# Two transitions between blocks: squares and weight-row products by halves, and both norms of the first from x and x times its row

## What is computed

```python
def rmsnorm(x, g):                      # rms_norm of the second part is the same
    y = xf * lax.rsqrt(jnp.mean(xf * xf, axis=-1, keepdims=True) + RMS_EPS)
    return (y * g.astype(jnp.float32)).astype(x.dtype)

# end of the first block: three gated branches, then
        x = x + jnp.einsum('bsd,de->bse', merged, w_out[l])
    return rmsnorm(x, final_g)

# second block, two layers
    for i in range(DEPTH_2):
        u = rms_norm(x, norm_pre[i])
        ...                             # layer 0: S5 and convolution, layer 1: gated linear attention
        x = x + rms_norm(y, norm_post[i])
    return x
```

## Time and profile before

| | |
|---|---|
| median of 3 runs | 1795.4 us |
| profiled execution | 1794.97 us, of it 1793.2 us span from the first to the last instruction |
| TensorE busy | 1667.4 us (93%) |
| VectorE busy | 928.9 us (52%) |
| ScalarE busy | 666.2 us (37%) |
| GpSimd busy | 203.4 us (11%) |
| mean granted TensorE clock | 0.972 of full speed |
| chain that ended last | PE 89%, DVE 4%, ACT 3% of the span |

### The profile page before, as it was taken

One profiled execution on the slowest core, in us unless ns is written; L12 is line 12 of the kernel. 1 busy time (PEld: TensorE's weight loads), 2 busy tenths in 40 slices (PEclk: granted clock), 3 DMA queues, 4 the chain that ended last, 5 costly groups with the idle time before them and its releaser, 6 DMA issues.

```text
span 1793.2 us, 20084 instructions
## 1 busy us (share of the span) xinstructions
PE 1667.4 (93%) x7876; PEld 1359.2 (76%) x7876; DVE 928.9 (52%) x1293; ACT 666.2 (37%) x920; POOL 203.4 (11%) x234
## 2 busy tenths in 40 slices
PE   6999989999999999989999989475989999999997
PEld 5887878878888888879988777354877778687775
DVE  4265264552246234558889937912464344453446
ACT  5333332223212223354544465216344334342442
POOL 4980000000000000031222202101000000000000
PEclk9999999999999999999999989797999999999999
DMA  8455433333333332257789838217422223132211
GB/s 245 127 155 152 131 94 94 94 117 106 99 101 94 94 98 102 95 211 161 145 216 195 162 132 187 48 62 184 131 60 64 78 71 105 48 104 60 82 48 59
DMA packets 151227, 206.75 MB, mean 115 GB/s; under 512 B 51963, under 2 KB 74987, under 8 KB 150123
## 3 DMA queue, kind: packets, MB, share of 16 engines
q1 hardware_dynamic: 131915, 173.62, 31.4%
q0 software_dynamic: 17568, 29.89, 10.2%
q10 hardware_dynamic: 1664, 2.13, 0.4%
HBM read 190.94 MB, written 14.68 MB: 115 GB/s over the span
## 4 chain that ended last, share of the span: by engine, by line
PE 89%; DVE 4%; ACT 3%; issue 2%; DMA 1%; SPq 0%; ACTq 0%; DVEq 0%
PE PS L2010 76%; PE PS L1988 2%; PE PS L2225 1%; PE PS L2277 1%; PE PS L2295 1%; PE PS L2164 1%; PE PS L2286 1%; PE PS L2131 1%; ACT XN L900 1%; DVE V L1391 1%; DMA WR<-in_conv_w_pw_dram 1%; PE PS L2194 1%; PE PS L2305 0%; DVE WL L1309 0%; PE PS L2179 0%
## 5 line engine op out<-in xcount | busy, mean ns | idle before, releaser
L2010 PE MATMUL PS<-HH,WH 128*128 128x512 f32 x1216 | 478.4, 393 | 10.5 <-issue 5.4
L2010 PE MATMUL PS<-HL,WH 128*128 128x512 f32 x1216 | 475.3, 391 | 0.0
L2010 PE MATMUL PS<-HH,WL 128*128 128x512 f32 x1216 | 475.2, 391 | 0.0
L893 ACT ACTIVATE WH<-WR 128x1024 fp32r<-128x1024 f32 x200 | 211.6, 1060 | 688.6 <-PE PS L2010 641.4
L1309 DVE TENSOR_TENSOR WL<-WR,WH 128x1024 fp32r<-128x1024 f32 x144 | 185.4, 1294 | 420.5 <-ACT WH L893 420.4
L2010 PEld LDWEIGHTS PS<-HH,WH 128*128 128x128 f32 x1216 | 229.7, 189 | 60.5 <-issue 10.8
L2010 PEld LDWEIGHTS PS<-HL,WH 128*128 128x128 f32 x1216 | 229.8, 189 | 48.2 <-issue 1.0
L2010 PEld LDWEIGHTS PS<-HH,WL 128*128 128x128 f32 x1216 | 229.4, 189 | 47.8
L2010 PE MATMUL PS<-WH,HH 128*128 128x512 f32 x384 | 153.2, 399 | 9.1 <-DVE WL L1309 4.2
L2010 PE MATMUL PS<-YH,WH 128*128 128x512 f32 x320 | 126.7, 396 | 36.0 <-DVE YL L1346 31.3
L1685 DVE SCALAR_TENSOR_TENSOR TMP<-CP,PRM,TMP 128x512 f32<-128x512 f32 x232 | 154.9, 740 | 0.0
(11 more groups left out here) (328 smaller groups left out, 1965.0 us busy)
## 6 DMA issues: line engine op xcount, KB each, us to landing
WR<-in_w_in_dram SPq DMA_DIRECT2D x96, 512.0 KB, 3.7
WR<-in_od_w_in_dram SPq DMA_DIRECT2D x32, 512.0 KB, 3.9
WR<-in_ev_w_in_dram SPq DMA_DIRECT2D x24, 512.0 KB, 3.9
WL<-in_ev_w_in_dram POOLq DMA_DIRECT2D x24, 512.0 KB, 7.5
WR<-in_ev_w_in_dram SPq DMA_DIRECT2D x32, 256.0 KB, 3.2
WR<-in_ev_w_out_dram SPq DMA_DIRECT2D x16, 512.0 KB, 4.2
WR<-in_od_w_in_dram SPq DMA_DIRECT2D x32, 256.0 KB, 3.4
WR<-in_od_w_out_dram SPq DMA_DIRECT2D x16, 512.0 KB, 3.8
```

Of the source, the lines that this page charges most:

```text
L893: act.activation(WH[:, n % RING, :, :], WR[:, n % RING, :, :], ACT.Copy).then_inc(w_hi, 1)
L2010: mm = pe.matmul(out_banks[m], st, mv, start=(kt == 0 and i == 0), stop=(kt == 2 * per - 1 and i == 2))
```

## The change

The first transition gets a second array `XG`, x times `FROW`. It is made by halves of 512 columns on VectorE (`weigh_x`), the first half of all four tiles right behind the four sums of the first half, ahead of the `split` of the unit's last chunk. ScalarE squares both X and `XG` by halves of 512, so that it has the sums of squares of x and of x times its row; both norms follow from them: X becomes XG over the root of mean(X^2) + eps, and XN1 is XG over the root of mean(XG^2) + eps * (mean(X^2) + eps). Sums of the first halves are turned into the biases of the later roots (rows 2, 3, 9 of the small array `XST`). `x1_norm` now makes both XN1 and X from `XG`, each with a reciprocal and one 128x1024 product. ScalarE's `split` (the `WH` of the next unit's chunk 0), which stood between the two norms of tile 3, now stands behind both.

The second transition squares YO by halves and makes YO times `PROW0` by halves (`weigh_y`), again with the four first halves ahead of the `split` of the last chunk; the product with rstd and the sum with X1 are one instruction. The norm of X1 is as before.

```diff
@@ -315,6 +315,10 @@
         AZ = put("AZ", "R4", [KT, SEQ])
         BZ = put("BZ", "R5", [KT, SEQ])
         XN2 = put("XN2", "R5", [TT, D])
+        XG = put("XG", "R2", [TT, D])
+        XST = put("XST", "SMALL", [10, TT])
+        JUNK1 = put("JUNK1", "YH", [TT, D])
+        JUNKG = put("JUNKG", "R5", [TT, D])
         MU = put("MU", "R6", [SEQ])
         RS = put("RS", "R6", [SEQ])
         ONES = put("ONES", "R6", [P], skip=2048)
@@ -421,6 +425,9 @@
             "o_sq", "o_std", "o_f", "o_hi", "o_lo", "rr_in", "st_done"))
         y2_zero = sem("y2_zero")
         sq5, std5, fin, fin_out, prow1_in = sem("sq5"), sem("std5"), sem("fin"), sem("fin_out"), sem("prow1_in")
+        xg_half, x_sums, x_base, x_left, x_sum = (sem(n) for n in (
+            "xg_half", "x_sums", "x_base", "x_left", "x_sum"))
+        yo_sums, yo_base = sem("yo_sums"), sem("yo_base")
         halves_done, y2_half, yg_done = sem("halves_done"), sem("y2_half"), sem("yg_done")
 
         def col(name, kt, n=1):
@@ -1083,13 +1090,34 @@
 
             load_sqrt()
             act.wait_ge(h_lo, 16)
+            def square(x, junk, row, t, sums):
+                act.activation(junk, x, ACT.Square, accum_out=XST[:, row, t:t + 1]).then_inc(sums, 1)
+
+            act.wait_ge(m_acc, 16)
+            for t in range(TT):
+                act.wait_ge(banks_dve, dve_after("w_out.0", t + 1))
+                square(X[:, t, 0:NC], XN1[:, t, 0:NC], 0, t, x_sums)
+                act.wait_ge(xg_half, t + 1)
+                square(XG[:, t, 0:NC], JUNKG[:, t, 0:NC], 1, t, x_sums)
+            act.wait_ge(x_sums, 2 * TT)
+            act.activation(XST[:, 2, :], XST[:, 0, :], ACT.Copy, scale=1.0 / D, bias=RMS_EPS).then_inc(x_base, 1)
             for t in range(TT):
                 act.wait_ge(banks_dve, dve_after("w_out.1", t + 1))
-                rms_tile(X[:, t, :], t, XN1[:, t, :], sq1, std1)
+                square(X[:, t, NC:D], XN1[:, t, NC:D], 4, t, x_sum)
+                act.wait_ge(x_sum, 2 * t + 1)
+                act.wait_ge(x_base, 2)
+                act.activation(XST[:, 6, t:t + 1], XST[:, 4, t:t + 1], ACT.Identity, scale=RMS_EPS / D,
+                               bias=XST[:, 3, t:t + 1]).then_inc(x_left, 1)
+                act.wait_ge(xg_half, TT + t + 1)
+                square(XG[:, t, NC:D], JUNKG[:, t, NC:D], 5, t, x_sum)
+                act.wait_ge(x_left, t + 1)
+                act.wait_ge(x_sum, 2 * t + 2)
+                act.activation(XST[:, 7, t:t + 1], XST[:, 5, t:t + 1], ACT.Sqrt, scale=1.0 / D,
+                               bias=XST[:, 6, t:t + 1]).then_inc(std2, 1)
+                act.activation(XST[:, 8, t:t + 1], XST[:, 4, t:t + 1], ACT.Sqrt, scale=1.0 / D,
+                               bias=XST[:, 2, t:t + 1]).then_inc(std1, 1)
                 if t == TT - 1:
                     split(1)
-                act.wait_ge(x1_done, t + 1)
-                rms_tile(X[:, t, :], t, XN1[:, t, :], sq2, std2)
             split(1)
             turned("u_t.0", 0, "norm_pre0")
             split(2)
@@ -1188,11 +1216,20 @@
                     act.activation(HH[:, kt, :], BZ[:, kt, :], ACT.Copy).then_inc(h_hi, 1)
             split()
             load_sqrt()
+            w0 = 16 * transfers(N_STATIC - RING) + 32
             act.wait_ge(h_lo, 40)
-            w0 = 16 * transfers(N_STATIC - RING) + 32
+            for t in range(TT):
+                act.wait_ge(banks_dve, dve_after("ev_b.0", t + 1))
+                square(YO[:, t, 0:NC], JUNK1[:, t, 0:NC], 0, t, yo_sums)
+            act.wait_ge(yo_sums, TT)
+            act.activation(XST[:, 2, :], XST[:, 0, :], ACT.Copy, scale=1.0 / D, bias=RMS_EPS).then_inc(yo_base, 1)
+            act.wait_ge(yo_base, 1)
             for t in range(TT):
                 act.wait_ge(banks_dve, dve_after("ev_b.1", t + 1))
-                rms_tile(YO[:, t, :], t, XN2[:, t, :], sq3, std3)
+                square(YO[:, t, NC:D], JUNK1[:, t, NC:D], 4, t, yo_sums)
+                act.wait_ge(yo_sums, TT + t + 1)
+                act.activation(STAT[:, 1, t:t + 1], XST[:, 4, t:t + 1], ACT.Sqrt, scale=1.0 / D,
+                               bias=XST[:, 2, t:t + 1]).then_inc(std3, 1)
                 if t == TT - 1:
                     hsplit(N_STATIC, 0, 1, w0)
                 act.wait_ge(x2_done, t + 1)
@@ -1568,22 +1605,36 @@
             done("w_out.0")
             for t in range(TT):
                 dve.tensor_tensor(X[:, t, 0:NC], bank("w_out.0", t), X[:, t, 0:NC], ALU.add).then_inc(banks_dve, 1)
+            dve.wait_ge(frow_in, 16)
+            dve.wait_ge(y_hi, 24)
+
+            def weigh_x(t, u):
+                dve.wait_ge(banks_dve, dve_after(f"w_out.{u}", t + 1))
+                dve.tensor_tensor(XG[:, t, u * NC:(u + 1) * NC], X[:, t, u * NC:(u + 1) * NC], FROW[:, u * NC:(u + 1) * NC],
+                                  ALU.mult).then_inc(xg_half, 1)
+
+            for t in range(TT):
+                weigh_x(t, 0)
             split(1)
-            dve.wait_ge(frow_in, 16)
+            dve.wait_ge(x_base, 1)
+            seq.inc(dve.tensor_scalar(XST[:, 9, :], XST[:, 2, :], RMS_EPS, None, ALU.mult))
+            seq.wait()
+            dve.scalar_tensor_tensor(XST[:, 3, :], XST[:, 1, :], 1.0 / D, XST[:, 9, :], ALU.mult, ALU.add).then_inc(x_base, 1)
 
             def x1_norm(t):
-                dve.wait_ge(std2, t + 1)
-                rstd_tile(t)
-                dve.tensor_scalar(XN1[:, t, :], X[:, t, :], STAT[:, 3, t:t + 1], None, ALU.mult).then_inc(xn1, 1)
+                for row, s, out, inc in ((7, std2, XN1, xn1), (8, std1, X, x1_done)):
+                    dve.wait_ge(s, t + 1)
+                    seq.inc(dve.reciprocal(XST[:, row, t:t + 1], XST[:, row, t:t + 1]))
+                    seq.wait()
+                    dve.wait_ge(xg_half, TT + t + 1)
+                    dve.tensor_scalar(out[:, t, :], XG[:, t, :], XST[:, row, t:t + 1], None, ALU.mult).then_inc(inc, 1)
 
             for t in range(TT):
                 tile_done("w_out.1", t, 0)
                 dve.tensor_tensor(X[:, t, NC:D], bank("w_out.1", t), X[:, t, NC:D], ALU.add).then_inc(banks_dve, 1)
+                weigh_x(t, 1)
                 if t:
                     x1_norm(t - 1)
-                dve.wait_ge(std1, t + 1)
-                rstd_tile(t)
-                dve.scalar_tensor_tensor(X[:, t, :], X[:, t, :], STAT[:, 3, t:t + 1], FROW[:, :], ALU.mult, ALU.mult).then_inc(x1_done, 1)
             split(1)
             x1_norm(TT - 1)
             split(1)
@@ -1768,8 +1819,17 @@
             done("ev_b.0")
             for t in range(TT):
                 dve.tensor_tensor(YO[:, t, 0:NC], bank("ev_b.0", t), YO[:, t, 0:NC], ALU.add).then_inc(banks_dve, 1)
+            dve.wait_ge(prow0_in, 16)
+
+            def weigh_y(t, u):
+                dve.wait_ge(banks_dve, dve_after(f"ev_b.{u}", t + 1))
+                seq.inc(dve.tensor_tensor(XN2[:, t, u * NC:(u + 1) * NC], YO[:, t, u * NC:(u + 1) * NC],
+                                          PROW0[:, u * NC:(u + 1) * NC], ALU.mult))
+
+            dve.wait_ge(weights_used, used_after("ev_b.0"))
+            for t in range(TT):
+                weigh_y(t, 0)
             split(1)
-            dve.wait_ge(prow0_in, 16)
             dve.wait_ge(x1_in, 16)
 
             def x2_norm(t):
@@ -1780,13 +1840,12 @@
             for t in range(TT):
                 tile_done("ev_b.1", t, TT - 1)
                 dve.tensor_tensor(YO[:, t, NC:D], bank("ev_b.1", t), YO[:, t, NC:D], ALU.add).then_inc(banks_dve, 1)
+                weigh_y(t, 1)
                 if t:
                     x2_norm(t - 1)
                 dve.wait_ge(std3, t + 1)
                 rstd_tile(t)
-                seq.inc(dve.scalar_tensor_tensor(YO[:, t, :], YO[:, t, :], STAT[:, 3, t:t + 1], PROW0[:, :], ALU.mult, ALU.mult))
-                seq.wait()
-                dve.tensor_tensor(X1[:, t, :], X1[:, t, :], YO[:, t, :], ALU.add).then_inc(x2_done, 1)
+                dve.scalar_tensor_tensor(X1[:, t, :], XN2[:, t, :], STAT[:, 3, t:t + 1], X1[:, t, :], ALU.mult, ALU.add).then_inc(x2_done, 1)
             hsplit(N_STATIC, 0, 1)
             x2_norm(TT - 1)
             hsplit(N_STATIC, 1, 1)
```

## The result

| | us, median (range) | mean | runs |
|---|---|---|---|
| before | 1795.71 (1794.92 to 1800.61) | 1796.96 | 9 |
| after | 1803.42 (1798.36 to 1806.42) | 1803.09 | 9 |

The changed kernel takes 1.0034 times as long, 95% interval 1.002 to 1.0049. The forecast was 1798.6, the range 1796.0 to 1801.8: the sign was right, the time lies outside. The profiled execution after took 1806.42 us (span 1804.7), the slowest of the nine and 3.3 us above their mean; its TensorE had a mean granted clock of 0.966 (before 0.972).

What follows compares the result with a forecast made beforehand. It took TensorE to bound the kernel (89% of the chain), with its waits for VectorE as the places that count. +2.9 (first transition), +0.05 (second) and +0.25 (clock) gave +3.2 us, 1798.6 us, range 1796.0 to 1801.8.

Steps and rivals of the forecast that it cites:

- Part 1: Tile 0 of both units: four first-half products ahead of the last chunk's `WL` make TensorE wait 2.35 us each time.
- 2.76 us for four products by the emptied pipe: VectorE ahead of `WL`: products holding it 4 x 0.69 us each time, sum 0.7 us higher; the prediction's row spoke against it.
- Part 2: Rest of the first transition, from tile 3's last sum: the next unit starts at T + 10.85, not T + 10.29, +0.55 us.
- Part 3: Rest of the second transition: unit starts at T + 8.17, not T + 10.42; 2.25 us won, +0.05 us net with its new wait.
- Part 4: TensorE's clock at the two new waits and the second exit: likeliest balance about +0.25 us.
- first item: Tile 0 of both units: the clock falls behind each new wait with chance 4 in 10, 1.7 us lost each.
- second item: Second exit: the clock stays up behind the shorter wait with chance one half, gaining 1.45 us.
- every other stage should only be shifted: All stages outside tile 0 and the exits: the same durations, only later in time.
- Clock falls behind the new waits: Rival at tile 0 of both units: 1.7 to 3.4 us on top of the fixed 2.95, 1800 to 1801.8 us; chance 0.38.
- Later `x1_done`: Rival: SyncE's write of X and eight weight loads start 2.6 us late; without cover 1801.2 us; chance 0.06.
- Cover: Rival in tile 0: TensorE has work ahead of chunk 3, so the waits don't come, -3.15 us, 1792.2 us; chance 0.05.
- does little: Rival: VectorE's waits for sums hide the products, both ends move by less than 1 us, 1795.9 us; chance 0.04.

Runs made afterwards that it cites:

- e1: The changed kernel with the last chunk's `WL` ahead of the four first-half products in both transitions; 1797.78 us, ratio 1.0006.
- e5: The changed kernel with nine extra matmuls on TensorE in the new wait of tile 0; 1801.86 us, ratio 1.0032.
- e16: The changed kernel run again without any edit; 1802.96 us, ratio 1.0037 to the kernel before.
- e13: e5 with 18 repeated transposes of tile 2 ahead of tile 3's at both exits; 1798.4 us, ratio 1.0014.
- e2: Only the first transition changed, the second as in the kernel before; 1802.57 us, ratio 1.0033.
- e4: The kernel before with four unused 128x512 products ahead of the last chunk's `WL` in both transitions; 1805.11 us, ratio 1.0042.
- e14: The changed kernel with 18 repeated transposes of tile 2 ahead of tile 3's at both exits, the tile 0 waits left open; 1802.17 us, ratio 1.0035.
- e3: Only the second transition changed, the first as in the kernel before; 1797.26 us, ratio 1.0006.
- e6: The changed kernel with `WL` first, tile 3's XN1 and first `HL` moved forward, and in the second transition tile 2's norm behind tile 3's X1; 1793.58 us, ratio 0.9984.
- e19: The kernel before with four unneeded 512-column products on VectorE ahead of the first transition's first `HL`; 1800.73 us, ratio 1.0029.
- e8: e1 with tile 2's transposes repeated 18 times ahead of tile 3's at both exits; 1793.4 us, ratio 0.9981.
- e15: e6 with eight repeated transposes of tile 2 ahead of tile 3's at the second exit alone; 1792.47 us, ratio 0.998.
- e17: The kernel before with one unneeded 512-column product on VectorE ahead of the first transition's first `HL`; 1798.22 us, ratio 1.0018.

## Why the prediction was wrong, step by step

- **Part 1, right.** Forecast 2.35 us twice; with the clock up, tile 0 to 3 takes 24.09 in place of 21.71 and 21.75 (+2.38, +2.34), and e1 takes both away. The rows show 2.11 us of idle time, just under the 2.2 to 2.5 that the prediction named as its sign, because a row counts it from the end of the matmul before. The 2.76 us for four products by the emptied pipe did not come: 759.11 to 761.51 is 4 x 0.60. The Trainium skill, VectorE: DVE Perf Modes, section The DRAIN you can't avoid, has an exception that the prediction left out: a next operation that is not held starts earlier. The rows agree with the exception. ScalarE's first-half squares make tile 0's sum 0.2 us late and not 1.6: with no fall of the clock (e5) it stands 765.39 - 757.31 = 8.08 us behind the first sums, before 760.57 - 755.11 = 5.46, and 2.38 are the wait. It costs nothing, as forecast.
- **Part 2, right:** +0.55 forecast, 10.87 - 10.29 = +0.58. **Part 3, right:** -2.25 forecast, 8.21 - 10.42 = -2.21. The sum of the fixed terms was 2.95 and is 3.1.
- **Part 4, the step that failed.** It put the clock's balance at +0.25 us; mean less fixed is +3.0 (+3.9 in e16), with an interval of 2.3 each. That this is the clock is shown by e13: with TensorE kept busy in the waits, 4 to 5 us of the changed kernel's mean go, and its fixed terms stay. Its first item holds: "4 in 10" for a fall behind each new wait, at 1.7 us. Of ten such waits in six profiles, of after, e16, e2, e4, e14 and e3 (e2 has only the first, e3 only the second), five had a fall: four of the five first ones, one of the five second ones, at 25.68 - 24.09 = 1.59 us.
- Its second item fell: the second exit "stays up one half" and gains 1.45. In the six profiles with this exit short and unfilled the rest was 461.73 (e3), 461.89 (e5), 462.26 (e6), 462.88 (e16), 463.87 (e1) and 464.17 us (after), never clearly below before's 461.74. Only with the wait filled is it less. The clock did not stay up in any of the six: the traces have it low for 3.4 us there in e3, e5 and e6 and for 6.8 in the other three. Before, part of the low stretch lay on idle time and cost nothing; the shorter exit took that idle time away.
- What it put at nothing without a reason: "every other stage should only be shifted". Being shifted was the trouble. Between the transitions the changed kernel lost 2.8 and 2.9 us in its two profiles, which are the slowest executions of their sets, so its mean loss there is likely less; it was not measured.
- The profile after adds up: start +1.60 (code before the change, an execution's luck), fixed +3.09, fall in tile 0 +1.59, between +2.79, rest +2.43, in all 11.5 (1806.42 - 1794.97 = 11.45). This is one slow execution against one fast one; the means differ by 6.1.
- **Rivals.** "Clock falls behind the new waits" (1800 to 1801.8) came nearest and was part of it, but it had only some of the places: with those waits filled (e5) 2.8 us are still left. "Later `x1_done`" did not come: from the first unit's start to the first sixteen transposes behind its matmuls took 883.84 - 793.26 = 90.58 us, before 90.92. Cover and "does little" are out by the waits seen. The range took the sum of chances at the waits named. With the untouched places it would have had to reach to about 1806: an estimate, 1794.97 plus the fixed 2.95, two falls of 1.6, and the 2.8 and 2.4 of between and rest in the profile after.

Open: how the executions of a kernel are spread over the beat, which one profile of each doesn't show, and with it why e19's surplus is 1.5; and by how much the two items of Part 4 and the place on the beat each enter the mean of 3.0.

## What to carry to other kernels

An instruction put ahead of one for which TensorE waits is paid in full; ask of every moved line what is queued behind it, and e1's swap of two statements took the wait away. Where TensorE has short waits all along, a change of a microsecond or two also moves every later wait against the beat on which the clock falls and rises; here that was worth 1 to 3 us. Take that into the range, cut both profiles into the same pieces, and look for pieces that changed without an edit. A wait of TensorE made shorter does not bring the clock back, and the slow stretch may then lie on dense matmuls: the second exit's 2.21 us were won, but the 1.45 us hoped for on top were not. A few repeated transposes in the wait, as in e8, e13 and e15, are a cheap way to see what the clock is worth.

## What the runs showed of the hardware

- The length of a wait does not decide whether the granted clock falls behind it: the same 2.40 us were followed by sixteen transposes in 1.94 us (before, e17) and in 2.58 (after).
- Repeated 128x128 transposes kept the clock up as well: with 18 of them in the wait of the second exit, the unit behind it began at the full rate (e13: 0.40 us for a matmul; after: 0.63).
- At the second exit after, the clock stayed at 0.50 for 6.80 us although TensorE worked for 6.17 us of them.
- Identical code up to the first sums took 754.58 to 757.40 us in twenty executions, and nine or more runs of one kernel lie 2 to 8 us apart (e15: eleven within 2.24 us; after: nine within 8.06). A difference of 2 us can be seen in such a kernel only over many runs.
